# Up part of the narrow feed-forwards as three 256-column products into the same PSUM columns, without the copy and the sum of two halves

## What is computed

```
def swiglu(x, w_gate, w_up, w_down):
    return (jax.nn.silu(x @ w_gate) * (x @ w_up)) @ w_down

D_MODEL = 1024; SEQ = 256; D_FF = FFN_HIDDEN = 2816
x = x + 0.5 * swiglu(rmsnorm(x, ffn1_norm[l]), ffn1_w_gate[l], ffn1_w_up[l], ffn1_w_down[l])
...
x = x + 0.5 * swiglu(rmsnorm(x, ffn2_norm[l]), ffn2_w_gate[l], ffn2_w_up[l], ffn2_w_down[l])
```

## Time and profile before

| | |
|---|---|
| median of 3 runs | 2416.15 us (2416.05 to 2418.61) |
| span of the profiled execution | 2415.3 us |
| PE busy | 2351.8 us (97%), 13342 products and as many weight loads |
| DVE busy | 1569.9 us (65%) |
| ACT busy | 1146.0 us (47%) |
| mean granted clock of PE | 0.992 of full speed |
| weights stream | 338 chunks of 1024 KB, 4.8 us from issue to landing |

### The profile page before, as it was taken

One profiled execution on the slowest core, in us unless ns is written; L12 is line 12 of the kernel. 1 busy time (PEld: TensorE's weight loads), 2 busy tenths in 40 slices (PEclk: granted clock), 3 DMA queues, 4 the chain that ended last, 5 costly groups with the idle time before them and its releaser, 6 DMA issues.

```text
span 2415.3 us, 33011 instructions
## 1 busy us (share of the span) xinstructions
PE 2351.8 (97%) x13342; PEld 1974.4 (82%) x13342; DVE 1569.9 (65%) x2355; ACT 1146.0 (47%) x1701; POOL 13.1 (1%) x43
## 2 busy tenths in 40 slices
PE   6999999999999999999999999999999999999998
PEld 4887787888888887888888887888888888778887
DVE  4686434656656677666766568676676665776766
ACT  4212222435533345445544568554454446784444
POOL 0000000000000000000000000000000000000000
PEclk8999999999999999999999999999999999999999
DMA  7467322323521224655455644355555555344553
GB/s 302 185 239 272 122 88 98 129 88 122 183 95 71 88 88 158 227 192 176 176 190 191 223 156 145 136 178 189 191 177 189 191 185 209 140 147 159 194 192 137
DMA packets 57919, 399.66 MB, mean 165 GB/s; under 512 B 7789, under 2 KB 8309, under 8 KB 10280
## 3 DMA queue, kind: packets, MB, share of 16 engines
q1 hardware_dynamic: 52704, 383.80, 43.7%
q10 hardware_dynamic: 4272, 10.08, 1.2%
q0 software_dynamic: 800, 3.73, 0.5%
HBM read 396.53 MB, written 2.63 MB: 165 GB/s over the span
## 4 chain that ended last, share of the span: by engine, by line
PE 85%; ACT 6%; DVE 6%; DMA 2%; issue 1%; SPq 0%; DVEq 0%; ACTq 0%
PE pair L506 81%; DMA ring<-in_stream 2%; DVE ring_parts L2287 1%; PE pair L901 1%; DVE ring_parts L2297 1%; ACT arena L1912 1%; ACT mix_high L1562 1%; ACT ring_high L1549 1%; PE pair L884 1%; PE pair L1039 1%; ACT arena L1950 0%; ACT arena L1949 0%; PE pair L1294 0%; DVE rows L2414 0%; PE pair L619 0%
## 5 line engine op out<-in xcount | busy, mean ns | idle before, releaser
L506 PE MATMUL pair<-xT_parts,ring_high 128*128 128x512 f32 x2112 | 747.9, 395 | 3.8 <-DVE ring_parts L2287 1.1
L506 PE MATMUL pair<-xT_parts,ring_parts 128*128 128x256 f32 (+2 forms) x2448 | 693.3, 298 | 8.0 <-DVE ring_parts L2297 5.0
L2287 DVE TENSOR_TENSOR ring_parts<-ring,ring_high 128x2048 fp32r<-128x2048 f32 x194 | 444.1, 2292 | 142.5 <-ACT ring_high L1549 142.5
L506 PEld LDWEIGHTS pair<-xT_parts,ring_parts 128*128 128x128 f32 (+1 forms) x2448 | 460.1, 188 | 51.9 <-issue 12.8
L506 PEld LDWEIGHTS pair<-xT_parts,ring_high 128*128 128x128 f32 x2112 | 384.5, 188 | 81.7 <-DVE ring_parts L2287 2.6
L1549 ACT ACTIVATE ring_high<-ring 128x2048 fp32r<-128x2048 f32 x198 | 377.3, 1909 | 67.7 <-DMA ring<-in_stream 67.6
L2297 DVE TENSOR_TENSOR ring_parts<-ring,mix_high 128x1024 fp32r<-128x1024 f32 x144 | 168.4, 1218 | 74.9 <-ACT mix_high L1562 74.6
L1600 ACT ACTIVATE arena<-pair 128x512 f32<-128x512 f32 x110 | 65.5, 596 | 260.9 <-PE pair L506 260.9
L506 PE MATMUL pair<-ring_parts,xT_parts 128*128 128x512 f32 (+1 forms) x448 | 176.3, 393 | 0.4 <-DVE rows L2527 0.2
L506 PE MATMUL pair<-mix_high,xT_parts 128*128 128x512 f32 (+1 forms) x576 | 173.7, 385 | 0.0
L1562 ACT ACTIVATE mix_high<-ring 128x1024 fp32r<-128x1024 f32 x144 | 143.2, 1048 | 62.3 <-DMA ring<-in_stream 59.8
(11 more groups left out here) (417 smaller groups left out, 3886.6 us busy)
## 6 DMA issues: line engine op xcount, KB each, us to landing
ring<-in_stream SPq DMA_DIRECT2D x338, 1024.0 KB, 4.8
xn<-in_mods SPq DMA_DIRECT2D x14, 1024.0 KB, 4.9
arena<-in_mods SPq DMA_DIRECT2D x14, 1024.0 KB, 4.8
arena<-in_bT ACTq DMA_DIRECT2D x1, 1536.0 KB, 9.0
bias_scratch<-bias_row POOLq DMA_DIRECT2D x1, 1536.0 KB, 8.6
X<-in_x ACTq DMA_DIRECT2D x1, 1024.0 KB, 11.9
X<-in_ctx ACTq DMA_DIRECT2D x1, 1024.0 KB, 16.4
arena<-in_bT ACTq DMA_DIRECT2D x1, 1024.0 KB, 7.4
```

What stands on the lines that cost most here:

```text
L506: m = pe.matmul(o, l, r, start=start, stop=stop)
L2287: dve.tensor_tensor(out=ring_r[:, slot].rearrange("p a b -> p (a b)"), in0=w, in1=high[:, slot, :], op=ALU.subtract).then_inc(low_ready, 1)
```

## The change

The narrow up part makes three products of 256 columns into the same 256 columns for each half and slice, in place of one of 512 and one of 256. Copy and sum fall away; silu reads the gate bank, or in raw feed-forwards a new buffer `scaled` that DVE writes as gate bank times `rootB`; the product reads the up bank. The semaphore `both_done` is now raised by the product after silu, so that is what gives the pair of banks back.

```
-        cross = room(3072, 2, 2, S)
-        both = room(4096, 2, 2, S)
+        scaled = room(3072, 2, S)
...
-                            elif k == 0:
-                                mm(o[:, :], wh, xT_r[:, k, :], True, False)
-                                mm(o[:, 0:T], wl, xT_r[:, k, 0:T], False, False)
                             else:
-                                mm(o[:, 0:T], wl, xT_r[:, k, 0:T], False, False)
-                                mm(o[:, :], wh, xT_r[:, k, :], False, k == KD - 1, inc)
+                                mm(o[:, 0:T], wl, xT_r[:, k, 0:T], k == 0, False)
+                                mm(o[:, 0:T], wh, xT_r[:, k, T:2 * T], False, False)
+                                mm(o[:, 0:T], wh, xT_r[:, k, 0:T], False, k == KD - 1, inc)
...
-                def cross_copy(f):
-
-                    act.wait_ge(up_full, c.f + f + 1)
-                    if f >= 2:
-                        act.wait_ge(both_done, c.f + f - 1)
-                    act.activation(cross[:, f % 2, :, :], pair[f % 2][:, :, S:2 * S], ACT.Copy).then_inc(cross_done, 1)
-
                 def gate(f):
 
                     if raw:
                         c.scaled += 1
                         act.wait_ge(gate_scaled, c.scaled)
                     else:
-                        act.wait_ge(both_done, c.f + f + 1)
+                        act.wait_ge(up_full, c.f + f + 1)
                     if f >= 2:
                         act.wait_ge(g_done, c.f + f - 1)
-                    act.activation(sil2[:, f % 2, :], both[:, f % 2, 0, :], ACT.Silu).then_inc(sil_done, 1)
+                    act.activation(sil2[:, f % 2, :], scaled[:, f % 2, :] if raw else pair[f % 2][:, 0, 0:S],
+                                   ACT.Silu).then_inc(sil_done, 1)
...
-                def both_sum(f):
-
-                    dve.wait_ge(cross_done, c.f + f + 1)
-                    dve.tensor_tensor(out=both[:, f % 2, :, :], in0=pair[f % 2][:, :, 0:S], in1=cross[:, f % 2, :, :],
-                                      op=ALU.add).then_inc(both_done, 1)
-                    if raw:
-                        dve.wait_ge(both_done, c.f + f + 1)
-                        if f == 0:
-                            c.raw += 1
-                            dve.wait_ge(root_out, c.raw)
-                        gate_ = both[:, f % 2, 0, :]
-                        dve.tensor_tensor(out=gate_, in0=gate_, in1=rootB, op=ALU.mult).then_inc(gate_scaled, 1)
+                def gate_scale(f):
+
+                    dve.wait_ge(up_full, c.f + f + 1)
+                    if f == 0:
+                        c.raw += 1
+                        dve.wait_ge(root_out, c.raw)
+                    dve.tensor_tensor(out=scaled[:, f % 2, :], in0=pair[f % 2][:, 0, 0:S], in1=rootB,
+                                      op=ALU.mult).then_inc(gate_scaled, 1)
 
                 def product(f):
 
                     dve.wait_ge(sil_done, c.f + f + 1)
-                    fstep(dve.tensor_tensor(out=gf[:, f % 2, :], in0=sil2[:, f % 2, :], in1=both[:, f % 2, 1, :],
-                                            op=ALU.mult))
+                    dve.tensor_tensor(out=gf[:, f % 2, :], in0=sil2[:, f % 2, :], in1=pair[f % 2][:, 1, 0:S],
+                                      op=ALU.mult).then_inc(both_done, 1)
+                    dve.wait_ge(both_done, c.f + f + 1)
```

More of the change, by code:

```diff
@@ L266, in build @@
         up_full = sem("up_products")
-        cross_done = sem("cross_terms_copied")
-        both_done = sem("gate_and_up_summed")
+        both_done = sem("gate_and_up_taken")
         sil_done = sem("sil_done")
@@ L1638, in ffn @@
                     elif what == "up":
-                        cross_copy(i)
                         if raw and i == 0:
@@ L2376, in ffn @@
                     elif what == "up":
-                        both_sum(i)
+                        if raw:
+                            gate_scale(i)
                         product(i)
```

## The result

The changed kernel takes 2435.19 us (median of 6 runs, 2429.86 to 2439.55), the kernel before 2415.76 us (6 runs, 2410.79 to 2418.61). The ratio is 1.0077, with a 95% interval of 1.0067 to 1.0087: 0.8% slower. The profiled execution took 2433.72 us with a span of 2432.0, which is 16.7 more than before's 2415.3, at the same granted clock (0.993 of full speed, 0.992 before). So the two traces can be laid side by side and the 16.7 us looked for. (The medians differ by 19.4 us. The executions of one kernel lie up to 10 us apart, so a few us of either difference are chance.)

What follows compares the result with a forecast made beforehand. PE, busy 97% of the span, was taken as the bound. Pace 14.3, a start stall 2.0 and other raw starts 0.2 gave +16.5 us on 2416.15, so 2432.6 us (0.7% slower), range 2423.5 to 2438.5.

Steps and rivals of the forecast that it cites:

- The pace, +14.3 us: Narrow up tiles: each of 1760 steps (one half and slice) takes 0.0081 us longer on PE, +14.3 us.
- I take a value between these two, 0.3575: Up-tile triple put between the sampled mean 0.3584 (+15.9 us) and an even mix of levels 0.3567 (+12.8 us).
- Half and half: Up-tile triples guessed to spend equal time at the levels 0.3533 and 0.3600: 0.3567 each, +12.8 us.
- A fixed time for each product does [explain it]: PE stream: each product takes 0.0131 us beyond its columns, so the added one costs about 0.0106 at the slow level.
- The bank given back later: Up tile 2, second narrow feed-forward: PE waits for the product behind silu instead of the sum, +2.0 us once.
- their +0.2: Up tile 2 at the three other raw starts: PE waits at most 0.1 us more each, +0.2 us together.
- Nothing behind them is late, since DVE and ACT run on as before: After the second narrow feed-forward's start stall: later products queue behind PE's wait, with no further lateness; no size given.
- What is removed and costed at nothing: 110 copies on ACT and 110 sums on DVE (65.5 and 75.7 us), already hidden by the PE stream: 0 us.
- The engines' work slowed PE: Without copy and sum the whole up part runs at the fast level: 2425 us, inside the forecast's 0.85 chance.
- Faster than before: PE keeps the repeated weights in a triple, which falls to about 0.347: 2414 us, chance 0.03.
- No change: An added product in the up part costs 0.0015 us or less: +4.8 us with stalls, 2421 us, chance 0.05.
- Slower still: PE's queue runs dry or stalls reach later tiles; at 0.365 a triple, 2446 us, chance 0.07.

Runs made afterwards that it cites:

- The split product alone: Kernel before with each 512-column product of the narrow up part cut into two of 256, copy and sum kept: 2434.52 us, ratio 1.0068.
- four products: Changed kernel with the 256-column product of the low weights cut into two of 128 columns: 2607.7 us, ratio 1.0784.
- half a load: Changed kernel, low-weight product put in the middle and loading only 64 of 128 weight columns: 2414.05 us, ratio 0.9994.
- fewer columns: Changed kernel with the product of high weights by low x on 128 of its 256 columns, full loads: 2415.85 us, ratio 0.9999.
- the rescaling moved later: Kernel before with DVE's rescaling of X (L2387) in the second narrow feed-forward after item 5 instead of item 1: 2414.02 us, ratio 0.9988.

## Why the prediction was right, and where its steps were not

The prediction was 2432.6 us; 2435.19 were measured, 2.6 more and inside the range of 2423.5 to 2438.5. The direction and the cause that carried it, PE's own pace, held. Its terms did not all, and that the sum came so near is in part luck. It had 14.3 + 2.0 + 0.2 = 16.5; between the two spans the traces have 18.1 for the pace, 2.0 for the stall and 1.2 for the down products, less 1.5 and 1.2 for waits of before that are gone, 1.2 at the starts and 0.7 in parts that the change doesn't touch, 16.7. So a pace 3.8 too small and a term that was missing were made up for by relief that the prediction put at nothing, by less growth at the starts and by chance in the parts that the change doesn't touch. (The top of the range, 2438.5, also stands 1.3 above its own bound of 2437.2, where 1 was meant for the spread, and the bottom has no such margin.)

- **The pace, +14.3 us.** Measured: 0.3597 - 0.3494 = 0.0103 a step and +18.1 us. The step that was mis-sized is "I take a value between these two, 0.3575": the triple was always at the slow level, 0.3600, of the earlier trace rows, and that bound (+18.7) was within 0.6 us. The split product alone shows that this is the price of the added product and of nothing else in the change. The fast triples, 12 in 4.24 us from 1350.74, stand in the changed kernel's trace at the same place, again 12 in 4.24 us, so that level belongs to this stretch and isn't a matter of chance. Half and half rested on nothing but the two levels of another step, that of 512 and 256 columns.
- **"A fixed time for each product does [explain it]".** This mechanism fell. It gave the right size for the third product, 0.0106, because its line was drawn through 512 and 256 columns, and a triple lies at the end of that line. At four products it was wrong by 0.087 us. What the runs show in its place: a stream of products with full loads of 128 weight columns doesn't go faster than one each 0.115 or 0.116 us on the mean, though a single product can follow another after 0.060. Three of those are 0.345 to 0.349; 768 columns at 2.4 GHz are 0.320, and run at 0.350 when one load is halved. In the triple the two limits all but meet, and the measured time is somewhat above both. In the step before, two loads (0.23) are far under 0.35, and the columns are the larger part of it; the rest also goes with the loads in part, by the two kernels with half a load in that step. That the length of the loads is what holds the triple up is shown by half a load, four products and fewer columns together; what inside load and issue takes the 0.115 us isn't, nor what makes up the 0.030 that remain above the columns.

  The Trainium skill, page "TensorE: Matmul & The Clock Gate", section "LDWEIGHTS (loading the stationary operand)", gives a load P / 1.2 ns, 107 ns for P = 128 columns. If loads alone set the pace, four products would take 0.43 us by it, an estimate. The trace has 0.460 for four, so a load, with whatever lies between two of them, takes somewhat longer than the page says. That a load of half the columns is shorter agrees with the page's P: its row is 0.14 us long instead of 0.19, and 64 columns fewer are 0.053 us by the page, an estimate. The section that the prediction cites, "Back-to-back issue gap" of the same page of the Trainium skill, gives its 2.5 ns for a product by itself and says that in a stream the load and the product both set the distance. The stream here agrees with the latter.
- **The bank given back later, +2.0 us at the second narrow feed-forward.** The wait was forecast by its chain, row by row, at about 2.7 us and is 2.75; the stretch grew by 2.0. At the three other raw starts PE doesn't wait at all, so their +0.2 is nothing.
- **"Nothing behind them is late, since DVE and ACT run on as before".** Nothing behind was late, but they don't run on as before: before, DVE was late for the chunk of up tile 4, and now its own work has become less and PE comes later. 1.5 us of the 2.0 came back some 18 us later (1159.18 in the earlier trace rows to 1177.40). That less work ahead of the chunk is enough is shown by the rescaling moved later; what the stall itself has to do with it isn't shown. The prediction read the trace up to the wait, and not for where the next wait of the same engine was.
- **"What is removed and costed at nothing".** It was worth 1.2 us at two turns to the norm and has a share in the 1.5. Copy and sum taken away alone, stall and all, give 0.9989 (0.9979 to 0.9998). So small, but not nothing: the earlier trace rows did show the 1.1 us for DVE's L2287.
- **The down products** went from 5.445 to 5.47 us between two pairs of up tiles, together +1.2 us, which the prediction hadn't. The split product alone has it too (5.47), copy and sum alone taken away has not (5.445), so it belongs to the products.
- **The rivals.** *The engines' work slowed PE*: against it are the split product alone (0.3597 with all the work) and copy and sum alone (0.3494 without it). *Faster than before*, weights kept: the triple at 0.3597, the same in an order without the repeat, and as many loads as products on every page speak against it. *No change*: 0.0103 a product, not 0.0015. *Slower still*: the stream never ran dry, and no pair of up tiles is above 11.52.

Open are what makes the two levels of the earlier trace rows (0.3533 and 0.3600), of which the up tiles took only the slow one, why the down products need a few starts to come back to their pace, and the parts of the 0.115 us.

## What to carry to other kernels

Where TensorE is the bound, count its products and the weight columns that they load, not only the columns that they multiply: cutting a product in two to save work on engines that weren't the limit cost 0.0103 us each time, and cutting once more cost 0.100. Look in the trace for a stretch that has the new shape already; its slower level was the answer to 0.6 us, while a line through other shapes holds only as far as the rows that it was drawn through. And where a change adds a wait, follow the waiting engine to its next wait: what the stall costs may be what it would have lost there.

## What the runs showed that was not expected

- A stream of products with full weight loads takes at least 0.115 to 0.116 us for each, on the mean: 0.460 for four (128, 128, 256 and 256 columns), 0.3488 for three with 640 columns. Single starts in it are 0.060 to 0.171 us apart.
- Loading 64 instead of 128 weight columns gives back 0.0097 us in a triple of 256-column products, and in a step of 512 and 256 columns 0.0033 (the load of the 256) or 0.0081 (that of the 512). The latter are not zero, although two loads fill but two thirds of the step: the load costs the stream something even where it seems to lie under it.
- Two products in a row with the same weights cost as much as with different ones, since each loads them anew.
- Short stretches at half the granted clock, at other places in each execution, move a span by some us: 1.4 us for each 3.4 us of them in the mixes.
